# Attention outputs: transposes in place of the merging matmuls, halves added on VectorE, scaling on GpSimd

## What is computed

```python
o_a = dense_attention(qa, ka, kva[..., QK_NOPE:])          # kind A, 6 heads: all keys
o_b = dilated_sliding_attention(rope(q), rope(k), v)       # kind B, 6 heads: banded, three dilations
o_c = neighbourhood_attention(q, k, v, rpb[l])             # kind C, 4 heads: a window on a 16 x 64 grid
x = x + concat(rms_norm(o_a), rms_norm(o_b), rms_norm(o_c)) @ w_out[l]
x = x + square(relu(rms_norm(x) @ w_mlp_in[l])) @ w_mlp_out[l]
```

## Time and profile before

| | |
|---|---|
| median of 3 runs | 2895.31 us (2893.7 to 2895.71) |
| profiled execution | 2891.39 us |
| its span, first to last instruction | 2889.5 us |
| mean granted TensorE clock | 0.996 |
| attention of layer 0, of layer 1 | about 290 to 640 us, about 1716 to 2066 us |

### The profile page before, as it was taken

One profiled execution on the slowest core, in us unless ns is written; L12 is line 12 of the kernel. 1 busy time (PEld: TensorE's weight loads), 2 busy tenths in 40 slices (PEclk: granted clock), 3 DMA queues, 4 the chain that ended last, 5 costly groups with the idle time before them and its releaser, 6 DMA issues.

```text
span 2889.5 us, 39557 instructions
## 1 busy us (share of the span) xinstructions
PE 2835.9 (98%) x14576; PEld 2424.2 (84%) x14576; DVE 1716.7 (59%) x2966; ACT 1043.4 (36%) x1912; POOL 141.3 (5%) x253
## 2 busy tenths in 40 slices
PE   8999999999999999999999999999999999999998
PEld 7998888878888888888798988888788888888886
DVE  6642878885545545455667348788745545545557
ACT  5332777873211111111234237777732111111113
POOL 0001230000000000000000013200000000000000
PEclk9999999999999999999999999999999999999999
DMA  5656774322111111111146577733211111111111
GB/s 198 197 179 216 183 187 106 92 72 81 44 44 44 52 50 44 44 58 51 53 177 210 181 203 180 174 92 88 73 66 44 58 44 44 56 46 44 44 62 70
DMA packets 150612, 285.30 MB, mean 99 GB/s; under 512 B 15056, under 2 KB 104784, under 8 KB 140752
## 3 DMA queue, kind: packets, MB, share of 16 engines
q1 hardware_dynamic: 139856, 254.16, 29.1%
q0 software_dynamic: 10624, 29.41, 3.6%
HBM read 210.60 MB, written 72.88 MB: 98 GB/s over the span
## 4 chain that ended last, share of the span: by engine, by line
PE 88%; DVE 5%; issue 3%; ACT 2%; DVEq 1%; DMA 1%; ACTq 0%; SPq 0%
PE ps L1491 24%; PE ps L1306 21%; PE ps L1506 18%; PE ps L1386 8%; PE ps L1400 6%; PE ps L1432 5%; PE ps L1442 2%; PE ps L1266 1%; PE ps L1425 1%; DVE x L1219 1%; PE ps L1348 1%; DVE vbuf L1206 1%; ACT rbuf L887 1%; PE ps L1377 1%; DVE hn L954 1%
## 5 line engine op out<-in xcount | busy, mean ns | idle before, releaser
L1506 PE MATMUL ps<-w_dn,hid 128*128 128x512 f32 x3072 | 713.0, 391 | 1.4
L1491 PE MATMUL ps<-hT,w_up 128*128 128x512 f32 x3072 | 702.5, 389 | 3.3 <-DVE hT L937 3.3
L1506 PEld LDWEIGHTS ps<-w_dn,hid 128*128 128x128 f32 x3072 | 573.6, 188 | 131.9 <-DVE x L1219 14.1
L1491 PEld LDWEIGHTS ps<-hT,w_up 128*128 128x128 f32 x3072 | 576.2, 188 | 123.1 <-ACT rbuf L887 3.8
L1306 PE MATMUL ps<-ws,hT 128*128 128x384 f32 (+3 forms) x2688 | 517.1, 351 | 6.9 <-DVE hT L937 5.3
L1306 PEld LDWEIGHTS ps<-ws,hT 128*128 128x128 f32 x2688 | 464.0, 190 | 38.8 <-DVE hT L937 5.8
L1219 DVE TENSOR_TENSOR x<-ps,x 128x512 f32<-128x512 f32 x512 | 342.7, 689 | 223.6 <-PE ps L1506 223.4
L1206 DVE TENSOR_TENSOR vbuf<-rbuf 128x512 f32<-128x512 f32 x128 | 88.6, 692 | 371.0 <-ACT rbuf L887 371.0
L837 ACT ACTIVATE pT<-ps 128x512 fp32r<-128x512 f32 (+1 forms) x448 | 240.3, 582 | 138.3 <-PE ps L1400 136.1
L937 DVE TENSOR_TENSOR pT<-ps,pT 128x512 fp32r<-128x512 f32 (+1 forms) x448 | 281.4, 664 | 6.7 <-ACT pT L837 5.8
L887 ACT ACTIVATE rbuf<-ps 128x512 f32<-128x512 f32 x128 | 76.6, 598 | 553.9 <-PE ps L1491 553.9
(11 more groups left out here) (87 smaller groups left out, 2247.6 us busy)
## 6 DMA issues: line engine op xcount, KB each, us to landing
raw<-in_wstream SPq DMA_DIRECT2D x76, 1024.0 KB, 4.8
head<-feats SPq DMA_DIRECT2D x192, 256.0 KB, 6.1
feats<-tst SPq DMA_DIRECT2D x128, 192.0 KB, 2.6
values<-vst POOLq DMA_DIRECT2D x32, 384.0 KB, 3.2
head<-values SPq DMA_DIRECT2D x24, 512.0 KB, 3.9
biasC<-in_bias_c SPq DMA_DIRECT2D x16, 768.0 KB, 11.4
raw<-in_wstream SPq DMA_DIRECT2D x12, 768.0 KB, 5.6
x_park<-x SPq DMA_DIRECT2D x16, 512.0 KB, 8.2
```

Of the source, the lines that this page charges most:

```text
L1491: last = pe.matmul(ps[:, k % 2, :], w_up[slot_of(l, 1 if first else 0)][:, w1, kt, ft * P:(ft + 1) * P], hT[:, w2, kt, sh * 512:(sh + 1) * ...
L1506: last = pe.matmul(ps[:, 2 + m % 4, :], hid[slot_of(l + 1, slot)][:, w1, ft, s * P:(s + 1) * P], w_dn[slot_of(l, 0 if last_group else 1)][ ...
```

## The change

For dense and grid blocks (`whole(b)`, blocks 0 to 19 of each layer) `merge` no longer adds the halves. It transposes the four 128x128 pieces of `oT` with the identity, and fills the whole bank. VectorE adds the two halves out of the bank with a reduction over pairs 64 columns apart, writes the unscaled sums to `O` or `oC`, and increments a new semaphore `o_sum`. GpSimd multiplies them by the reciprocals in place, and it is this product that increments `o_ready`. Dilated blocks stay as they were, but the first of them waits on VectorE until GpSimd's last product is done. GpSimd's transfers now stand between its products in the order of blocks: after the second block of a grid head come the loads for the next grid head, the 8 stores and the read back.

```diff
+WHOLE = sum(ITEMS[4 * b_][0] in "AC" for b_ in range(NB))
...
         def merged(b):
-            return ps[:, 4 if b == NB - 1 else 6 + b % 2, 0:4 * HD]
+            return ps[:, 4 if b == NB - 1 else 6 + b % 2, :]
+        def reciprocals(b):
+            return a_rd[:, 4 * b:4 * b + 4].unsqueeze(2).to_broadcast([P, 4, HD])
+        def output_of(b):
+            kind, h, q = ITEMS[4 * b]
+            return oC[h % 2][:, q:q + 4, :] if kind == "C" else O[:, q:q + 4, h * HD:(h + 1) * HD]
+        def whole(b):
+            return ITEMS[4 * b][0] in "AC"
...
                 grids = [n for n in range(NH) if HEADS[n][0] == "C"]
-                for n in grids:
-                    load_grid_values(l, n)
-                    if n > grids[0]:
-                        park_grid(l, n - 2)
-                        read_grid(l, n - 2)
-                park_grid(l, grids[-1])
-                read_grid(l, grids[-1])
+                load_grid_values(l, grids[0])
+                weighed = 0
+                for b in range(NB):
+                    if not whole(b):
+                        continue
+                    pool.wait_ge(o_sum, l * WHOLE + weighed + 1)
+                    weighed += 1
+                    pool.tensor_tensor(output_of(b), output_of(b), reciprocals(b), ALU.mult).then_inc(o_ready, 1)
+                    n = b // 2
+                    if n in grids and b % 2:
+                        if n < grids[-1]:
+                            load_grid_values(l, n + 2)
+                        park_grid(l, n)
+                        read_grid(l, n)
...
                     dve.reciprocal(a_rd[:, 4 * b:4 * b + 4], a_den[:, 4 * b:4 * b + 4])
-                    dve.drain()
-                    dve.tensor_tensor(o, merged(b).rearrange("p (t d) -> p t d", d=HD),
-                                      a_rd[:, 4 * b:4 * b + 4].unsqueeze(2).to_broadcast([P, 4, HD]),
-                                      ALU.mult).then_inc(o_ready, 1)
+                    if whole(b):
+                        dve.tensor_reduce(o, merged(b).rearrange("p (t w d) -> p t d w", w=2, d=HD), axis=AX.X, op=ALU.add)
+                        dve.drain().then_inc(o_sum, 1)
+                    else:
+                        dve.drain()
+                        if whole(b - 1):
+                            dve.wait_ge(o_ready, l * NB + b)
+                        dve.tensor_tensor(o, merged(b)[:, 0:4 * HD].rearrange("p (t d) -> p t d", d=HD),
+                                          reciprocals(b), ALU.mult).then_inc(o_ready, 1)
...
                         c = k * P + (b % 2) * 512
-                        last = pe.matmul(merged(b)[:, k * HD:(k + 1) * HD], oT[l % 2][:, c:c + P], pair[:, :],
-                                         start=True, stop=True)
+                        if whole(b):
+                            last = pe.transpose(merged(b)[:, k * P:(k + 1) * P], oT[l % 2][:, c:c + P], ident[:, :])
+                        else:
+                            last = pe.matmul(merged(b)[:, k * HD:(k + 1) * HD], oT[l % 2][:, c:c + P], pair[:, :],
+                                             start=True, stop=True)
```

More of the change, by code:

```diff
@@ L321, in encoder @@
         t_done, t_hi, t_lo = sem("t_done"), sem("t_hi"), sem("t_lo")
+        o_sum = sem("o_sum")
         pv_done, ot_ready, mg_done, o_ready = sem("pv_done"), sem("ot_ready"), sem("mg_done"), sem("o_ready")
```

## The result

The changed kernel takes **2942.44 us** (median of 4 runs, 2941.9 to 2945.6) against 2894.89 us of the kernel before on the same chip: ratio 1.0166, 95% interval 1.0154 to 1.0179, 47.6 us slower. The profiled execution has a span of 2940.1 us (before 2889.5) and a mean granted clock of 0.988 (before 0.996).

What follows compares the result with a forecast made beforehand. TensorE, busy 98% of the span with hardly a gap in attention, was taken to bound the kernel. Stalls 55.8, smaller meetings 0.4, clock 10.2, less 18.5 for merges, gave +47.9 on 2895.3: 2943 us, range 2926 to 2978.

Steps and rivals of the forecast that it cites:

- The stalls: Sums of blocks 6, 10 and 14, both layers: TensorE waits for GpSimd's signal, 9.3 us six times, +55.8 us.
- The chain: From VectorE's output of a grid head's last block through GpSimd's queue to the next block's product and signal: 18.7 us.
- The landing: GpSimd's wait for a grid head's stores before the read back: 1.67 us with DMA quiet, 5.54 as far end.
- TensorE: -18.5 forecast: Merges of 40 dense and grid blocks: transposes cost 0.36 us instead of 0.82, saving 0.46 us each.
- it costs nothing by itself: VectorE's reduction takes 0.27 us more than the product, 10.6 us over 40 blocks, but adds no kernel time.
- The cover I named: VectorE busy only 1.35 us of the 3 us following 342 us, hiding its longer operation; without it, 10.6 us.
- The clock: After each of six stalls TensorE runs at half clock, 1.7 us more each, +10.2 us; ends 0 and 3.4 each.
- Smaller meetings: Block 0's signal comes 0.2 us after TensorE would start block 2, twice: +0.4 us.
- Slow landing: Rival: the wait for the stores stays 5.54 us behind 16 loads, six times 3.87 us more, 2966 us; chance 0.15.
- Code for the product: Rival: GpSimd's first product must fetch code, delaying block 2's sums; 14 us gives 2957 us; chance 0.04.
- The transposes save nothing: Rival: transposes take two passes as before, so none of TensorE's 18.5 us is saved, 2962 us; chance 0.02.
- The queue doesn't decide: Rival: GpSimd's chain fits without stalls and TensorE's saving shows, 2877 us; chance 0.05.

Runs made afterwards that it cites:

- e12: The changed kernel with the drain behind VectorE's reduction removed, the reduction itself signalling `o_sum`; GpSimd's order unchanged: 2940.98 us, ratio 1.0162.
- e2: The changed kernel with GpSimd issuing the next grid head's 16 loads ahead of the product of the grid head's second block: 2913.87 us, ratio 1.0068.
- e4: The changed kernel with the 16 loads ahead of the second block's product and the read back behind the next block's product: 2885.05 us, ratio 0.9962.
- e5: e4 with the drain removed, VectorE's reduction itself signalling `o_sum`: 2876.68 us, ratio 0.9936.
- e13: The changed kernel with 32 idle matmuls ahead of the sums of blocks 6, 10 and 14, before the wait for grid values: 2933.33 us, ratio 1.0129.
- e10: e5 with VectorE's reduction itself freeing the PSUM bank, stores and norm waiting for GpSimd's products: 2877.69 us, ratio 0.9942.
- e1: The changed kernel with VectorE's reduction itself incrementing `o_ready`, GpSimd's products signalling a semaphore of their own: 2917.69 us, ratio 1.0072.
- e7: The changed kernel with the merging matmuls of before; VectorE only copies the sums out, GpSimd scales, same order: 2966.8 us, ratio 1.0247.

## Why the prediction was right, point by point

The forecast was 2943 us and its mechanism was the one that happened; but two terms were off by about 7 us each, in opposite directions. That the total is within 1 us is luck.

- **The stalls: +55.8 forecast, 48.9 measured.** Right in place, number and releaser. The chain was 18.7 us forecast, 18.29 measured (18.2 to 18.9 over the six): reduction 0.69 against 0.66, signal 0.30 against 0.10 (336.92 to 337.02, behind the drain), product 0.8 against 0.61, loads, stores and read as in the earlier trace rows, landing 1.67 against 1.70. Each stall is 8.15 us and not 9.3, mostly because TensorE comes later: it arrived 10.23 us after the output's start, not 9.44, since VectorE's longer hold had cost it its lead (without the drain, in e12, it arrives at 9.84 us). The shorter chain gives the other 0.3 us.
- **The landing.** 1.70, 2.33 and 1.68 us; the reading that it depends on how busy DMA is when the stores go out fits in both directions (5.32 us in e2), and 16 loads directly ahead did not make it long.
- **TensorE: -18.5 forecast, -11.2 measured.** The price of a merge was right, 0.35 us against 0.36 forecast. But the step "it costs nothing by itself", on VectorE's 0.27 us more, failed. I had charged only the longer operation and not the drain that moved behind it; together they hold VectorE's next operation 0.46 us longer than before (1.04 against 0.58 us from the reciprocal). The cover I named, free time in the 3 us stretch behind, is not what matters: the item's maxima are next in line and TensorE's transposes wait for them. e4 gained 10.3 us of the 18.5; e5, without the drain, 18.2. So the longer reduction alone did cost next to nothing, but there it held VectorE only 0.08 us more; what 0.27 us would have cost, no run shows.
- **The clock: +10.2 forecast, +11.9 measured** by the intervals behind the stalls (9.1 us in e13's total). Right in kind and size, but from kernel to kernel the same kind of stall cost from 1.5 to 4.2 us.
- **Smaller meetings: +0.4 forecast.** Nothing seen: GpSimd's first product ends at 307.68 us, 0.95 us before block 2's sums start at 308.63, and these wait for VectorE's `pT`.
- Measured terms, in the profiled execution: 48.9 of waits and 11.9 of half clock. From the first block's sums to the last's the two layers together take 49.6 us more than before, so 11.2 us of the merges' saving were realised. The whole execution has a span 50.6 us longer, and the medians differ by 47.6 us.
- The upper end of the range adds up to about 2975 us (2966 and half of 5.0 + 10.2 + 3.2), not 2977; nothing hangs on it.
- **The rivals.** *Slow landing* is excluded by the 1.70 us. *Code for the product*: GpSimd's first product ran at 307.07 us in 0.61 us, like all others, and no stall stands there: it cost nothing. Whether code was fetched in the 13.37 us that GpSimd was idle ahead of it, no row shows. *The transposes save nothing*: excluded by the record counts and the 0.35 us. *The queue doesn't decide* is excluded by the six waits and by e4; its 2877 us are what came once the queue was mended and the drain gone (e5 and e10). For the product's time the Trainium skill, "GPSIMD Engine Reference", section 3.1, gave an estimate of 0.56 us in the prediction; the trace has 0.614 us, nearer than the 0.8 that I took from rows of other engines.

## What to carry to other kernels

An engine that only issues transfers looks free at 5%, but whatever is signalled from it waits for everything queued ahead, here 15 us of issue and landing. Before giving it a signal that someone waits for, put the transfers where their issue ends before that signal is due, and any read that needs a landing behind it. Charge an added instruction on a busy engine by what it does to the start of the next one there, drains included (one that moves frees time where it stood and takes it where it stands), and ask who waits for that next one. A total that agrees with a forecast does not show that its terms do: compare the places where each term should appear.

## What the runs showed of the hardware that I had not expected

- A drain that carries the signal held VectorE's next operation back by 0.38 us (0.95 against 0.57) where a grid or dilated item came next and by 0.20 us (0.78 against 0.58) where a dense one did; 40 of them were worth 7.9 us. A drain between the reciprocal and the product put the product 0.24 us behind the reciprocal's start in the kernel before, where without one the reduction stands 0.09 us behind it.
- Waits of TensorE of 3 to 4 us were in most cases followed by half clock (e1: 0.59 in 352 to 355 us), but not in all: e2's first, 3.39 us, was followed by 1.00 throughout.
- How long the half clock lasts behind a stall varies between kernels whose stalls are equally long, and within one: 3.2 to 5.7 us of work in the changed kernel, 8.5 to 9.1 us in e7, and 3.2 against 6.3 us behind the second stall of the changed kernel and of e12. A forecast of this price has an end of at least 4.2 us a stall, more than the 3.4 that I gave.
- 7.55 us of idle matmuls in a stall kept the clock at 1.00, and each took 0.236 us where nobody waited for TensorE.
